# A ring of 512 points with the far pairs on VectorE, and a Fourier channel table with its high and low columns side by side

## The chip, the cores and the metric

The kernel runs on one core of a Trainium2 chip. The metric is the device time of one execution in microseconds (us), the median of three runs. TensorE is called PE here, its weight loads PEld; VectorE is DVE, ScalarE is ACT, GpSimd is POOL, SyncE is SP.

## The reference

One layer mixes 272 positions (16 learned meta tokens and 256 tokens) of width 2048. A wide projection feeds three branches of 1024 channels each; the branches are gated, projected back, weighted, summed, projected once more and added to the input, and a last RMSNorm follows. Branch A and branch B are what the change touches:

```python
def fftconv(v, kf, skip):                       # branch A, twice in a row
    L = v.shape[1]
    vf = jnp.fft.rfft(v.astype(jnp.float32), n=2 * L, axis=1)
    y = jnp.fft.irfft(vf * kf[None], n=2 * L, axis=1)[:, :L]
    return y + v.astype(jnp.float32) * skip.astype(jnp.float32)

def hyena_mixer(u, x1, x2, kf, skip):
    z = fftconv(u, kf[:, 0], skip[0])
    z = x1.astype(jnp.float32) * z
    z = fftconv(z, kf[:, 1], skip[1])
    z = x2.astype(jnp.float32) * z
    return z.astype(u.dtype)

def fourier_mixer(xb):                          # branch B, over 256 channels of a group and all positions
    B, L, C = xb.shape
    xg = xb.astype(jnp.float32).reshape(B, L, FN_GROUPS, C // FN_GROUPS)
    y = jnp.fft.fft2(xg, axes=(1, 3), norm='ortho').real
    return y.reshape(B, L, C).astype(xb.dtype)
```

The filter `kf` has 272 lags forward and 271 back. It comes from a small network over the positions, whose last layer `w4` gives 4096 columns, each multiplied by a decay `exp(-t * abs(decay))`. All is float32.

## The kernel before

**Number format.** PE multiplies numbers of a shorter format (F32R here). A float32 matrix is split into a high part, made by ACT (a copy into F32R), and a low part, made by DVE (the matrix less its high part). A product then takes three matmuls, high x high, low x high and high x low; the helper `three` issues them at L594 to L596, so these lines carry most of PE's work. The 16 rows or bins that go beyond 128 or 256 would need matmuls of their own; where they are rows of the contraction, their high, low and high parts are stacked under one another (rows 0, 32 and 64 of an 80-row tile) and one matmul covers them. The helper `stacked` issues it at L599.

**Main loop.** The channels go in 4 chunks of 256 (`c`), and a chunk has 20 steps (`t`). At each step one slab of projection weights (1 MB, loaded by SP into `raw`, four deep) is used: `split` makes `w_hi` on ACT and `w_lo` on DVE, two slabs ahead, and PE does 48 matmuls with it. Ten projections (`u`, `q`, `k`, `v`, `x1`, `x2`, three gates and the input of branch B) take two steps each. Between the slabs each engine has its share of the three branches at fixed places, written out by hand as `if t == ...` in one loop per engine; every engine works its list in that order and waits on semaphores. After the four chunks comes the merge: 512 columns wide, four blocks of 18 slabs, and the output projection with 16 slabs.

**Branch A.** The convolution is circular over a ring of 2 x 272 = 544 points, with 272 complex bins. For each of 8 groups `g` (2 per chunk, one per order of the convolution) the filter is made so: `make_h4(g, tt)` (L640, L641) runs the network's last layer for the lag tiles 0, 1 (128 lags each) and 2 (16 lags); `sum_and_difference` and `sd_low` on DVE and `envelope` and `sd_high` on ACT multiply it by the decay and split it; `filter_xy` transforms it to 256 bins, with a `stacked` matmul (out of `sd_rest`) for the 16 lags behind each `three`; `filter_f` (L669 to L674 and L599) makes the 16 bins that remain. The signal is folded (`fold`, DVE), transposed (`turn`, L717), transformed (`forward` for 256 bins, `forward_extra`, L736, L737 and L599, for the last 16), multiplied by the spectrum (`straight`, `crossed`, `spectrum_low` on DVE; f = 2 is the tile of 16 bins), and brought back (`inverse` with `wide_half`, L744 and L745, with one `stacked` matmul of 136 columns per accumulation for the 16 bins), then `unfold`.

**Branch B.** `fnet_channels(t, bank)` does the transform over channels by a table `fch` of cosines and sines with 130 columns per position tile (t = 0, 1): `three` matmuls for each half of the channels. `channels_high` (ACT) and `channels_low` (DVE) split the result, `fnet_tokens` transforms over positions.

**Where steps meet.** At t = 7 PE ends with `scores(0)` of the attention branch; DVE does `biased(c, 0)` on them, then `normalized(c, 0)` once ACT has taken exponentials, and copies the block `v` out of PSUM (L1632) during step 7 of its own list; PE transposes the probabilities (`turn_p`, L780, L782) and `v` (`turn`, L717) after the slab of t = 8. `crossed(2, 0, ...)` of the 16 bins stands ahead of `biased(c, 0)`, and its `spectrum_low` behind.

Of the kernel before, what the change touches and what calls it, by code (L numbers as in the profile page):

```python
# [35 lines left out]
L = 272  # L36
# [13 lines left out]
FFT_N = 2 * L  # L50
HL = L // 2

# [54 lines left out]
FPOS = np.concatenate([np.arange(256, L), np.arange(0, 256, 2), np.arange(1, 256, 2)])  # L107
FSTACK = 4 * 128 + 8 * NM
FWIDE = FSTACK + 4 * 128 + 2 * NM
# [24 lines left out]
def constants():  # L134

    pos = np.arange(L, dtype=np.float64)
    bins = np.concatenate([np.arange(128, 144), np.arange(128), np.arange(L - 1, 143, -1)]).astype(np.float64)
    om = TWO_PI * (bins + 0.5) / FFT_N
    sign = 1.0 - 2.0 * (bins % 2)

    half = (pos[:HL, None] + 0.5) * om[None, :]
    even = np.cos(half) + sign[None, :] * np.sin(half)
    odd = np.cos(half) - sign[None, :] * np.sin(half)
    none = np.zeros((HL - 128, L))
    back = [np.concatenate([even.T[p:p + n], odd.T[p:p + n]], axis=1) for p, n in TOK]
    hi, lo = two_parts(np.concatenate([even[:128], odd[:128], back[0], back[1]], axis=1),
                       np.concatenate([np.concatenate([even[128:], none]), np.concatenate([none, odd[128:]]), back[2]], axis=1))
    wide = [part[:, at:at + HL] for b in (2 * L, 3 * L) for part, at in ((hi, b), (lo, b), (hi, b + HL), (lo, b + HL))]
    extra_bins = [part[:, at:at + NM] for part in (hi, lo) for at in (0, L)]
    extra_rest = [np.pad(hi[:, at:at + NM], ((0, 0), (0, 2 * NM))) for at in (4 * L, 5 * L)]  # L150
    sym = (np.concatenate([hi[:, 0:2 * L]] + wide + [hi[:, 4 * L:]] + extra_bins + extra_rest, axis=1),
           lo[:, 0:2 * L])

    lag = FPOS.astype(np.float64)[:, None] * om[None, :]
    cosk, sink = np.cos(lag) / FFT_N, -np.sin(lag) * sign[None, :] / FFT_N
    first, extra = slice(NM, NM + 128), slice(0, NM)
    te, to, tr = slice(NM, NM + 128), slice(NM + 128, L), slice(0, NM)
    is_even = 1.0 - FPOS[tr, None] % 2
    filt = two_parts(np.concatenate([cosk[te, first], sink[te, first], cosk[to, first], sink[to, first],
                                     cosk[te, extra], sink[te, extra], cosk[to, extra], sink[to, extra]], axis=1),  # L160
                     np.concatenate([cosk[tr, first] * is_even, sink[tr, first] * is_even,
                                     cosk[tr, first] * (1.0 - is_even), sink[tr, first] * (1.0 - is_even),
                                     cosk[tr, extra], sink[tr, extra]], axis=1))

    hi, lo = filt
    more = [part[:, 512 + 2 * NM * tt:512 + 2 * NM * tt + 2 * NM] for tt in range(2) for part in (hi, lo)]
    filt = np.concatenate([hi[:, 0:512]] + more + [hi[:, 512 + 4 * NM:]], axis=1), lo[:, 0:512]
# [5 lines left out]
    fch = two_parts(np.concatenate([np.cos(ang), fsin], axis=1).reshape(2, 128, 2 * FK).transpose(1, 0, 2).reshape(128, -1), None)  # L173
# [16 lines left out]
    negt = np.zeros((128, 3), f32)  # L190
    for i, (p, n) in enumerate(TOK):
        negt[:n, i] = -t[FPOS[p:p + n], 0]
# [8 lines left out]
def build(nc, x, meta, w_stream, filt_in, sym_in, fch_in, ftok_in, net_in, negt_in, mask_in, ident_in, params_in, w4,  # L201
# [5 lines left out]
    def place(name, shape, dt=F32):  # L207
# [3 lines left out]
        return t  # L211


    params = place("params", [128, 128])
    ident = place("ident", [128, 128])
    negt = place("negt", [128, 3])
    mask = place("mask", [128, GRID_W])
# [118 lines left out]
    with ExitStack() as ctx:  # L336
# [253 lines left out]
        def _(pe):  # L590
# [34 lines left out]
            def make_h4(g, tt):  # L625
# [11 lines left out]
                if tt == 2:  # L637
                    pe.wait_ge(h4_read, 3 * g + 1)
# [1428 lines left out]
```

## Time and profile before

| | |
|---|---|
| runs of before | 1112.69, 1112.76, 1112.93 us (median 1112.76) |
| profiled execution: span from first to last instruction | 1111.3 us |
| profiled execution: around its span | the profile gives no time of its own for it; its span lies 1.46 us under the median |
| PE busy | 1092.6 us, 98% of the span, 7104 matmuls recorded |
| DVE busy | 785.6 us, 71% |
| ACT busy | 568.6 us, 51% |
| POOL busy | 67.0 us, 6% |
| DMA | 201.80 MB, mean 182 GB/s |

Matmuls overlap in the records: one lasts some 0.28 us from its start to its end, while the next starts after 0.11 to 0.23 us. What a matmul costs PE is therefore read from the distance between two starts, and not from its duration. Idle time of an engine costs something only where another engine waits for it; each instruction that had to wait carries the wait and what ended it.

### The profile page before, as it was taken

The page shows a single profiled execution, that of the slowest core. Times are in us where ns is not written, and L with a number is a line of the kernel's source. Part 1 is how long each engine was busy: PE and PEld are TensorE (multiplying, and loading weights), DVE is VectorE, ACT ScalarE, POOL GpSimd, SP SyncE. Part 2 cuts the span into 40 slices and gives each one's busy share as a digit, 9 for nine tenths or more (in the row PEclk, how much of TensorE's full clock was granted, in tenths as well). Part 3 has the DMA queues.
Part 4 walks back from the last instruction along what each step waited for, and adds up shares of the span by engine and source line. Part 5 has one row for each costly group of instructions (what it writes and reads, how often), then busy time and mean ns, then how long its engine had stood idle before and what let it go on. Part 6 is the DMA issues. An engine that isn't in the chain of part 4 may idle for free.

```text
span 1111.3 us, 17195 instructions
## 1 busy us (share of the span) xinstructions
PE 1092.6 (98%) x7104; PEld 1000.8 (90%) x7104; DVE 785.6 (71%) x1185; ACT 568.6 (51%) x794; POOL 67.0 (6%) x104
## 2 busy tenths in 40 slices
PE   5999999999999999999999999999999999999997
PEld 5999999999999999999999988888888888888886
DVE  7888888688897798986888785454555545554654
ACT  6755555456465556554655564444444444344543
POOL 5130000300003000002000000000000000000000
PEclk9999999999999999999999999999999999999999
DMA  9763443644344634354444575555555555557652
GB/s 353 253 189 123 152 145 131 208 171 150 117 161 165 205 124 152 132 175 178 149 140 149 187 252 192 197 183 198 200 199 184 197 190 189 189 190 269 223 192 111
DMA packets 30734, 201.80 MB, mean 182 GB/s; under 512 B 3905, under 2 KB 4289, under 8 KB 7969
## 3 DMA queue, kind: packets, MB, share of 16 engines
q1 hardware_dynamic: 25264, 180.34, 46.8%
q0 software_dynamic: 5248, 19.85, 5.5%
q8 instruction: 56, 0.92, 0.3%
q10 hardware_dynamic: 144, 0.52, 0.1%
q14 instruction: 22, 0.17, 0.1%
HBM read 195.46 MB, written 5.24 MB: 181 GB/s over the span
## 4 chain that ended last, share of the span: by engine, by line
PE 98%; DMA 1%; ACT 0%; SPq 0%; DVE 0%; issue 0%; ACTq 0%
PE ps L594 30%; PE ps L596 30%; PE ps L595 30%; PE ps L599 2%; PE ps L717 1%; PE ps L744 1%; DMA xin<-x 1%; PE ps L780 1%; PE ps L622 1%; PE ps L640 1%; PE ps L641 1%; PE ps L772 0%; PE ps L771 0%; PE ps L993 0%; PE ps L782 0%; PE ps L745 0%
## 5 line engine op out<-in xcount | busy, mean ns | idle before, releaser
L1413 DVE TENSOR_TENSOR w_lo<-raw,w_hi 128x1024 fp32r<-128x1024 f32 (+1 forms) x338 | 408.6, 1223 | 249.4 <-ACT w_hi L1051 247.4
L1051 ACT ACTIVATE w_hi<-raw 128x1024 fp32r<-128x1024 f32 x334 | 349.0, 1057 | 342.7 <-PE ps L596 341.6
L594 PE MATMUL ps<-xn_hi,w_hi 128*128 128x272 f32 (+2 forms) x1280 | 367.9, 287 | 0.0
L596 PE MATMUL ps<-xn_hi,w_lo 128*128 128x272 f32 (+2 forms) x1280 | 365.0, 285 | 0.0
L595 PE MATMUL ps<-xn_lo,w_hi 128*128 128x272 f32 (+2 forms) x1280 | 364.8, 285 | 0.0
L594 PEld LDWEIGHTS ps<-xn_hi,w_hi 128*128 128x128 f32 x1280 | 241.6, 189 | 2.5 <-DVE xn_lo L1468 0.4
L595 PEld LDWEIGHTS ps<-xn_lo,w_hi 128*128 128x128 f32 x1280 | 241.2, 188 | 0.7
L596 PEld LDWEIGHTS ps<-xn_hi,w_lo 128*128 128x128 f32 x1280 | 241.5, 189 | 0.0
L594 PE MATMUL ps<-w_hi,xg_hi 128*128 128x512 f32 x352 | 137.2, 390 | 0.0
L596 PE MATMUL ps<-w_hi,xg_lo 128*128 128x512 f32 x352 | 137.0, 389 | 0.0
L595 PE MATMUL ps<-w_lo,xg_hi 128*128 128x512 f32 x352 | 136.9, 389 | 0.0
L596 PEld LDWEIGHTS ps<-w_hi,xg_lo 128*128 128x128 f32 x352 | 66.1, 188 | 13.8
L595 PEld LDWEIGHTS ps<-w_lo,xg_hi 128*128 128x128 f32 x352 | 66.1, 188 | 13.6
L594 PEld LDWEIGHTS ps<-w_hi,xg_hi 128*128 128x128 f32 x352 | 66.1, 188 | 13.5
L594 PE MATMUL ps<-w_hi,yb_hi 128*128 128x512 f32 x192 | 74.8, 389 | 0.0
L596 PE MATMUL ps<-w_hi,yb_lo 128*128 128x512 f32 x192 | 74.7, 389 | 0.0
L595 PE MATMUL ps<-w_lo,yb_hi 128*128 128x512 f32 x192 | 74.7, 389 | 0.0
L1267 ACT ACTIVATE y_hi<-prod 128x512 fp32r<-128x512 f32 (+1 forms) x24 | 15.2, 632 | 70.2 <-DVE prod L1698 70.1
L594 PE MATMUL ps<-w_hi,m_hi 128*128 128x512 f32 x128 | 49.9, 390 | 0.0
L596 PE MATMUL ps<-w_hi,m_lo 128*128 128x512 f32 x128 | 49.8, 389 | 0.0
L595 PE MATMUL ps<-w_lo,m_hi 128*128 128x512 f32 x128 | 49.8, 389 | 0.0
L594 PEld LDWEIGHTS ps<-w_hi,yb_hi 128*128 128x128 f32 x192 | 36.0, 188 | 7.6 <-issue 0.2
(292 smaller groups left out, 1388.2 us busy)
## 6 DMA issues: line engine op xcount, KB each, us to landing
raw<-w_stream SPq DMA_DIRECT2D x167, 1024.0 KB, 4.9
branch_y<-ystage POOLq DMA_DIRECT2D x12, 256.0 KB, 4.0
y_raw<-branch_y POOLq DMA_DIRECT2D x3, 1024.0 KB, 7.1
xin<-x SPq DMA_DIRECT2D x2, 1024.0 KB, 6.4
w4s<-w POOLq DMA_DIRECT2D x16, 128.0 KB, 5.6
absd<-decay POOLq DMA_DIRECT2D x8, 256.0 KB, 5.8
h<-x POOLq DMA_DIRECT2D x2, 1024.0 KB, 8.3
rows_t<-rpb POOLq DMA_DIRECT2D x8, 219.0 KB, 6.2
```

The lines of the kernel that those rows point to most:

```text
L594: mm(out_ap, a_hi, b_hi, start=first, stop=False)
L595: mm(out_ap, a_hi, b_lo, start=False, stop=False)
L596: return mm(out_ap, a_lo, b_hi, start=False, stop=last)
L599: return mm(out_ap, a, b, start=first, stop=last)
L622: last = nc.tensor.transpose(ps[:, 4 + k % 4, p:p + 128], xin[:, t, 128 * k:128 * k + 128], ident[:, :])
L640: mm(out_ap, hid_s[:, p:p + n], w4_hi[:, :, :].rearrange("p d n -> p (d n)"), start=True, stop=False)
L641: mm(out_ap, hid_s[:, p:p + n], w4_lo[:, :, :].rearrange("p d n -> p (d n)"), start=False, stop=True).then_inc(h4_mm, 1)
L717: last = nc.tensor.transpose(dst, src[:, i, p:p + n], ident[:, :])
L744: mm(ps[:, bank, 0:L], y_hi[:, f, ri, chans], sym_hi[:, back:back + L], start=f == 0, stop=False)
L1051: A(w_hi[:, w % 2, part, :], raw[:, w % 4, 1024 * part:1024 * part + 1024], ACT.Copy).then_inc(hi_done, 1)
L1267: ins = A(y_hi[0:n, f, :, :], prod[0:n, 2, :, :], ACT.Copy)
L1413: return V.tensor_tensor(dst, src, hi.bitcast(F32), ALU.subtract)
```

## The change

Branch A goes over to a ring of 512 points. Then 256 bins do, and the last tile of 16 bins and its table columns disappear. On that ring the pairs of positions that are 256 to 271 apart wrap and would be counted at a wrong lag, so the ring's filter holds lags 0 to 255 only (`filter_xy` loses its `stacked` matmuls) and the far pairs are summed directly: 16 x 16 products on each side for every channel. `far_lags(g)` on PE (two matmuls for each of 4 outputs, of 32 columns, with a 128-column stationary operand out of `w4_hi` or `w4_lo`) makes the filter at 32 lags with channels on the partitions; `far_envelope` (ACT, 4 small exponentials, with the decay as a scale per partition) and `far_kernel` (DVE) weight it and add what the ring wrapped; `far_terms(order, src)` on DVE multiplies by a view of it shaped like a Toeplitz matrix (128 x 512) and sums along rows (a reduce of 512 elements to 32); `unfold` adds the 16 positions at either end. In order 1 only the later positions are needed.

In branch B the table's high and low columns stand side by side (`fch_two`, 260 wide), so the high part of the input takes one matmul of 260 columns in place of two of 130, into two ranges of the bank. Those two must be added: ACT copies one out of PSUM (`fch_sum`), DVE adds the other, and the split is made from the sum.

Tables loaded at the start change in size: `fch` doubles (1032 and 1040 columns where there were twice 516), `filt` goes from 1184 + 512 to 512 + 512 columns, `sym` from 2608 + 544 to 2112 + 512. ACT takes the absolute value of a 32-column block of `params` once, just behind `hid_s` and ahead of `envelope(0, 0)`, and DVE sets one column of `hid_s` to zero.

The diff, cut to what runs:

```diff
             def filter_xy(g):
-                pe.wait_ge(sdlo_done, 3 * g + 2)
+                pe.wait_ge(sdlo_done, 2 * g + 2)
                 pe.wait_ge(h4_read, 3 * g + 3)
                 for ri in range(2):
-                    into = [ps[:, 7 - tt, CC * ri:CC * ri + CC] for tt in range(2)]
                     for tt in range(2):
                         col = 256 * tt + 128 * ri
-                        three(into[tt], filt_hi[:, col:col + 128], filt_lo[:, col:col + 128], sd_hi[:, tt, ri, :],
-                              sd_lo[:, tt, ri, :], True, False)
-                    if ri == 0:
-                        pe.wait_ge(sdlo_done, 3 * g + 3)
-                    for tt in range(2):
-                        col = FSTACK + 256 * tt + 128 * ri
-                        last = stacked(into[tt], filt_hi[0:STACK, col:col + 128], sd_rest[0:STACK, ri, :], False, True)
+                        last = three(ps[:, 7 - tt, CC * ri:CC * ri + CC], filt_hi[:, col:col + 128], filt_lo[:, col:col + 128],
+                                     sd_hi[:, tt, ri, :], sd_lo[:, tt, ri, :], True, True)
...
+            def far_lags(g):
+                pe.wait_ge(h4_read, 3 * g + 1)
+                for d in range(2):
+                    for i in range(2):
+                        out_ap = ps[:, 6, 2 * NM * (2 * d + i):2 * NM * (2 * d + i) + 2 * NM]
+                        chans = slice(128 * i, 128 * i + 128)
+                        mm(out_ap, w4_hi[:, d, chans], hid_s[:, 0:2 * NM], start=True, stop=False)
+                        last = mm(out_ap, w4_lo[:, d, chans], hid_s[:, 0:2 * NM], start=False, stop=True)
+                last.then_inc(h4_mm, 1)
...
             def wide_half(bank, ri, chans):
                 for f in range(2):
...
-                rest = 8 * L + HL * ri
-                return stacked(ps[:, bank, 0:HL], y_hi[0:STACK, 2, ri, chans], sym_hi[0:STACK, rest:rest + HL], False, True)
...
             def fnet_channels(t, bank):
...
-                    last = three(ps[0:n, bank, cols], fi_hi[:, i, p:p + n], fi_lo[:, i, p:p + n], fch_hi[:, i, cols],
-                                 fch_lo[:, i, cols], i == 0, i == 1)
+                    at_ = 2 * (FK + 1) * t
+                    mm(ps[:, bank, 0:2 * (FK + 1)], fi_hi[:, i, p:p + n], fch_two[:, i, at_:at_ + 2 * (FK + 1)], start=i == 0, stop=False)
+                    last = mm(ps[:, bank, 0:FK + 1], fi_lo[:, i, p:p + n], fch_two[:, i, at_:at_ + FK + 1], start=False, stop=i == 1)
...
                     if t == 2:
-                        make_h4(2 * c + 1, 2)
+                        far_lags(2 * c + 1)
                     if t == 4:
                         filter_xy(2 * c + 1)
-                    if t == 5:
-                        filter_f(2 * c + 1)
...
-                    if t == 5:
-                        pe.wait_ge(y_full, c * 6 + 1)
-                        forward_extra()
...
+            def far_envelope(g):
+                if g:
+                    act.wait_ge(h4_read, 3 * g)
+                c, o_ = divmod(g, 2)
+                for d in range(2):
+                    for i in range(2):
+                        at_ = DEC + 8 * (2 * o_ + d) + 2 * c + i
+                        ins = A(far_env[:, d, i, :], negt[:, 2:2 + 2 * NM], ACT.Exp, scale=params[:, at_:at_ + 1])
+                ins.then_inc(env_done, 1)
...
+            def far_kernel(g):
+                o_ = g % 2
+                dve.wait_ge(env_done, 3 * g + 3)
+                dve.wait_ge(h4_mm, 3 * g + 3)
+                V.tensor_tensor(far[:, :, :, :].rearrange("p d i n -> p (d i n)"), ps[:, 6, 0:8 * NM],
+                                far_env[:, :, :, :].rearrange("p d i n -> p (d i n)"), ALU.mult).then_inc(h4_read, 1)
+                dve.wait_ge(h4_read, 3 * g + 3)
+                if g == 0:
+                    dve.wait_ge(far_zeroed, 1)
+                link(V.tensor_tensor(far_k[:, o_, :, :, NM - 1:2 * NM - 1], far[:, :, :, 0:NM], far[:, ::-1, :, NM:2 * NM], ALU.add))
...
+            def far_terms(order, src):
+                ins = V.tensor_tensor(far_p[:, 0, :, :, :], toeplitz(order, 0, True), spread(src, 0), ALU.mult)
+                if order:
+                    link(ins)
+                else:
+                    link(V.tensor_tensor(far_p[:, 1, :, :, :], toeplitz(order, 1, False), spread(src, NB), ALU.mult))
+                    link(V.tensor_reduce(far_y[:, 1, :, :], far_p[:, 1, :, :, :], mybir.AxisListType.X, ALU.add))
+                link(V.tensor_reduce(far_y[:, 0, :, :], far_p[:, 0, :, :, :], mybir.AxisListType.X, ALU.add))
...
             def channels_high(f, second):
                 if not second:
                     for r in range(2):
-                        half = slice(FK * r, FK * r + FK)
                         act.wait_ge(n1_mm, f * 3 + r + 1)
-                        A(p2_hi[:, r, half], ps[:, 4 + r, half], ACT.Copy).then_inc(n1_hi, 1)
+                        A(fch_sum[:, r, :], ps[:, 4 + r, FK + 1:2 * FK + 2], ACT.Copy).then_inc(n1_part, 1)
+                    for r in range(2):
+                        act.wait_ge(n1_sum, f * 2 + r + 1)
+                        A(p2_hi[:, r, FK * r:FK * r + FK], fch_sum[:, r, r:r + FK], ACT.Copy).then_inc(n1_hi, 1)
...
             def channels_low(f, second):
                 if not second:
                     for r in range(2):
+                        dve.wait_ge(n1_part, f * 2 + r + 1)
+                        V.tensor_tensor(fch_sum[:, r, :], fch_sum[:, r, :], ps[:, 4 + r, 0:FK + 1], ALU.add).then_inc(n1_sum, 1)
+                    for r in range(2):
                         dve.wait_ge(n1_hi, f * 3 + r + 1)
...
                     if t == 6:
-                        crossed(2, 0, straight(c, 2, 0))
                         biased(c, 0)
-                        spectrum_low(c, 2, 0)
+                        far_terms(0, u)
                         normalized(c, 0)
...
                     if t == 13:
-                        crossed(2, 1, straight(c, 2, 1))
                         turned(c * HC + 4, pt_hi, pt_lo, pT_lo[:, :, :], pT_hi[:, :, :], pT_rest, 6, NG, 32)
                         attended(c, 2)
-                        spectrum_low(c, 2, 1)
+                        far_terms(1, x1)
```

What stands on PE behind the slab of t = 5 in the first chunk before (`filter_f`, then `forward_extra`), between two slabs' matmuls:

```order
L596 MATMUL ps<-xn_hi,w_lo 128x272
L669 MATMUL ps<-sd_hi,filt_hi 48x256
L670 MATMUL ps<-sd_lo,filt_hi 16x256
L599 MATMUL ps<-sd_rest,filt_hi 16x256
L673 MATMUL ps<-sd_lo,filt_hi 16x256
L674 MATMUL ps<-sd_hi,filt_hi 48x256
...
L736 MATMUL ps<-uT_hi,sym_hi 48x256
L737 MATMUL ps<-uT_lo,sym_hi 16x256
L599 MATMUL ps<-uT_hi,sym_hi 48x256
...
L594 MATMUL ps<-xn_hi,w_hi 128x272
```

In the changed kernel nothing is left there: the slab of t = 6 follows that of t = 5. The new matmuls on PE stand behind the slab of t = 2, where before the two of the 16-lag tile stood (`w_hi` and `w_lo` are `w4_hi` and `w4_lo` by the names here); the changed kernel has there:

```order
L593 MATMUL ps<-xn_hi,w_lo 128x256
L645 MATMUL ps<-hid_s,w_hi 128x32
L646 MATMUL ps<-hid_s,w_lo 128x32
L645 MATMUL ps<-hid_s,w_hi 128x32
L646 MATMUL ps<-hid_s,w_lo 128x32
...
L591 MATMUL ps<-xn_hi,w_hi 128x256
```

Two matmuls of 512 columns became eight of 32 columns, each with its own weights.

On DVE at t = 6 of the first chunk, before (L1744 is `biased`, L1751 and L1753 are `normalized`, L1632 is the copy of `v`):

```order
L1687 TENSOR_TENSOR extra<-extra,ps 16x512
L1691 TENSOR_TENSOR prod<-extra,kspec 16x512
L1696 TENSOR_TENSOR prod<-extra,kspec 16x512
L1697 TENSOR_TENSOR prod<-prod 16x256
L1698 TENSOR_TENSOR prod<-prod 16x256
...
L1747 TENSOR_SCALAR stat<-stat 128x2
L1413 TENSOR_TENSOR y_hi<-prod,y_hi 16x512
L1751 RECIPROCAL stat<-stat 128x2
L1753 TENSOR_SCALAR sco<-sco,stat 128x272 x2
L1413 TENSOR_TENSOR w_lo<-raw,w_hi 128x1024
L1632 COPY v<-ps 128x544
```

and in the changed kernel:

```order
L1703 TENSOR_SCALAR stat<-stat 128x2
L1512 TENSOR_TENSOR far_p<-far_k,u 128x512
L1516 TENSOR_TENSOR far_p<-far_k,u 128x512
L1517 TENSOR_REDUCE far_y<-far_p 128x32
L1518 TENSOR_REDUCE far_y<-far_p 128x32
L1707 RECIPROCAL stat<-stat 128x2
L1709 TENSOR_SCALAR sco<-sco,stat 128x272 x2
L1359 TENSOR_TENSOR w_lo<-raw,w_hi 128x1024
L1595 COPY v<-ps 128x544
```

Five instructions ahead of `biased` are gone, and the one between `biased` and `normalized` has become four.

## Rows read from the trace of the kernel before

**Rows 1.** The profile's page: busy time of the engines, and the chain that ended last.

```profile
PE 1092.6 (98%) x7104; PEld 1000.8 (90%) x7104; DVE 785.6 (71%) x1185; ACT 568.6 (51%) x794; POOL 67.0 (6%) x104
...
PE 98%; DMA 1%; ACT 0%; SPq 0%; DVE 0%; issue 0%; ACTq 0%
```

**Rows 2.** The waits of PE: us in total, times, longest.

```profile
PE ps L610 <- DMA net<-net_in: 7.6, 1, 7.6
PE ps L834 <- ACT ps L1063: 3.9, 1, 3.9
```

**Rows 3.** Busy time by stretch, the second chunk; behind POOL the granted clock (PEclk).

```profile
207.00:354.00 147.00, 147.00 (x1205) 145.45 (x1204) 124.01 (x226) 83.40 (x136) 10.37 (x17) 1.00 0.47 158
```

**Rows 4.** Timeline of PE at `filter_f`, first and last start (start, duration in us).

```profile
209.06 0.28 PE L669 MATMUL ps<-sd_hi,filt_hi 128*48 128x256 f32 x1
...
210.24 0.29 PE L594 MATMUL ps<-xn_hi,w_hi 128*128 128x272 f32 x1
```

**Rows 5.** Timeline of PE at `forward_extra`.

```profile
246.82 0.28 PE L736 MATMUL ps<-uT_hi,sym_hi 128*48 128x256 f32 x1
...
247.53 0.29 PE L594 MATMUL ps<-xn_hi,w_hi 128*128 128x272 f32 x1
```

**Rows 6.** Timeline of PE at the 16-lag tile of `make_h4`.

```profile
222.90 0.40 PE L640 MATMUL ps<-w_hi,hid_s 128*16 128x512 f32 x1
...
223.37 0.28 PE L594 MATMUL ps<-xn_hi,w_hi 128*128 128x256 f32 x1
```

**Rows 7.** Timeline of PE at one pair of `stacked` matmuls in `filter_xy`.

```profile
236.46 0.41 PE L599 MATMUL ps<-sd_rest,filt_hi 80*128 80x256 f32 x2
236.71 0.28 PE L594 MATMUL ps<-sd_hi,filt_hi 128*128 128x256 f32 x1
```

**Rows 8.** Timeline of PE in `inverse`, a run of 136-column matmuls.

```profile
124.79 0.27 PE L599 MATMUL ps<-sym_hi,y_hi 80*128 80x136 f32 x1
...
125.01 0.28 PE L595 MATMUL ps<-sym_hi,y_hi 128*128 128x136 f32 x1
```

**Rows 9.** Groups by form on PE: busy us, mean ns of one.

```profile
L745 PE MATMUL ps<-sym_hi,y_lo 128*128 128x136 f32 x48 | 10.9, 226 | 0.0
...
L596 PE MATMUL ps<-sym_hi,y_lo 128*128 128x136 f32 x16 | 4.4, 276 | 0.0
```

**Rows 10.** Groups by form of weight loads: 128 and 16 stationary columns.

```profile
L596 PEld LDWEIGHTS ps<-sym_hi,y_lo 128*128 128x128 f32 x16 | 3.1, 192 | 0.0
...
L596 PEld LDWEIGHTS ps<-fch_hi,fi_lo 128*16 128x16 f32 x8 | 0.8, 95 | 0.2
```

**Rows 11.** Groups by form on DVE, a product of 512 elements in SBUF.

```profile
L1880 DVE TENSOR_TENSOR u<-u,x 128x512 f32<-128x512 f32 x4 | 2.7, 685 | 0.0
```

**Rows 12.** Timeline of DVE at t = 6 and 7, second chunk.

```profile
261.69 0.17 DVE L1747 TENSOR_SCALAR stat<-stat 128x2 f32<-128x2 f32 x1
...
263.41 0.17 DVE L1751 RECIPROCAL stat<-stat 128x2 f32<-128x2 f32 x1 [0.46 <-ACT sco L1275]
263.61 0.63 DVE L1753 TENSOR_SCALAR sco<-sco,stat 128x272 f32<-128x272 f32 x2
264.37 1.23 DVE L1413 TENSOR_TENSOR w_lo<-raw,w_hi 128x1024 fp32r<-128x1024 f32 x1
265.51 0.72 DVE L1632 COPY v<-ps 128x544 f32<-128x544 f32 x1
```

**Rows 13.** Timeline of PE there: behind `scores(0)`, and `turn(v)`.

```profile
260.13 0.29 PE L594 MATMUL ps<-xn_hi,w_hi 128*128 128x272 f32 x1
...
266.83 0.71 PE L717 MATMUL ps<-ident,v 128*128 128x128 f32 x5
```

**Rows 14.** Timeline at the start, DVE's low part of slab 4.

```profile
47.22 1.22 DVE L1413 TENSOR_TENSOR w_lo<-raw,w_hi 128x1024 fp32r<-128x1024 f32 x1
```

**Rows 15.** Timeline of PE there, the first matmul with slab 4.

```profile
48.59 0.36 PE L594 MATMUL ps<-xn_hi,w_hi 128*128 128x272 f32 x1
```

**Rows 16.** Groups by form on ACT, its smallest copy of all 128 partitions.

```profile
L1220 ACT ACTIVATE k_hi<-k_hi 128x64 fp32r<-128x64 f32 x4 | 1.0, 257 | 0.1
```

More of the change, by code:

```diff
@@ L49 @@
 HID, EMB = 64, 33
[L50 removed]
+RING = 512
+NB = RING // 2
 HL = L // 2
+LF = L + NM
+HF = LF // 2
 TOK = [(NM, 128), (NM + 128, 128), (0, NM)]
@@ L136, in constants @@
     pos = np.arange(L, dtype=np.float64)
[L137 to L163, printed above, removed]
@@ L165, in constants @@
-    hi, lo = filt
-    more = [part[:, 512 + 2 * NM * tt:512 + 2 * NM * tt + 2 * NM] for tt in range(2) for part in (hi, lo)]
-    filt = np.concatenate([hi[:, 0:512]] + more + [hi[:, 512 + 4 * NM:]], axis=1), lo[:, 0:512]
+    bins = np.concatenate([np.arange(128), np.arange(NB - 1, 127, -1)]).astype(np.float64)
+    om = TWO_PI * (bins + 0.5) / RING
+    turn = np.where(bins < 128, 1.0, -1.0)
+    half = (pos[:HL, None] - (L - 1) / 2) * om[None, :]
+    even = np.cos(half)
+    odd = -np.sin(half) * turn[None, :]
@@ new lines, in constants @@
+    none = np.zeros((HL - 128, NB))
+    back = [np.concatenate([even.T[p:p + 128], odd.T[p:p + 128]], axis=1) for p in (0, 128)]
+    hi, lo = two_parts(np.concatenate([even[:128], odd[:128]] + back, axis=1),
+                       np.concatenate([np.concatenate([even[128:], none]), np.concatenate([none, odd[128:]])], axis=1))
+    wide = [part[:, at:at + HL] for b in (BACK, BACK + L) for part, at in ((hi, b), (lo, b), (hi, b + HL), (lo, b + HL))]
+    sym = np.concatenate([hi[:, 0:BACK]] + wide + [hi[:, BACK + 2 * L:]], axis=1), lo[:, 0:BACK]
@@ L169, in constants @@
+    lag = np.arange(NB, dtype=np.float64)[:, None] * om[None, 0:128]
+    cosk, sink = np.cos(lag) / NB, -np.sin(lag) / NB
+    filt = two_parts(np.concatenate([cosk[0::2], sink[0::2], cosk[1::2], sink[1::2]], axis=1), None)
     ch = np.arange(CC, dtype=np.float64)
@@ L172, in constants @@
     fsin[:, [0, FK - 1]] = 0.0
-    fch = two_parts(np.concatenate([np.cos(ang), fsin], axis=1).reshape(2, 128, 2 * FK).transpose(1, 0, 2).reshape(128, -1), None)
+    both = np.concatenate([np.cos(ang), fsin], axis=1).reshape(2, 128, 2 * FK).transpose(1, 0, 2)
+    hi, lo = two_parts(both.reshape(128, -1), None)
+    hi, lo = hi.reshape(128, 2, 2 * FK), lo.reshape(128, 2, 2 * FK)
+    pairs = [np.concatenate([part[:, :, cols] for part in (hi, lo)], axis=2) for cols in (slice(0, FK + 1), slice(FK - 1, 2 * FK))]
+    fch = np.concatenate(pairs, axis=2).reshape(128, -1), np.concatenate([hi, lo], axis=2).reshape(128, -1)
     angl = TWO_PI * ((pos[:, None] * pos[None, NM:]) % L) / L
@@ L659, in filter_xy @@
                         if ri == 1:
                             last.then_inc((kx_mm, ky_mm)[tt], 1)
-            def filter_f(g):
-                bank = 7
-                pe.wait_ge(kx_evac, g + 1)
-                for ri in range(2):
-                    out_ap, wide_ap = (ps[0:n, bank, CC * ri:CC * ri + CC] for n in (NM, 3 * NM))
-                    col, step = 512 + NM * ri, 4 * NM
-                    mm(wide_ap, filt_hi[:, col:col + 3 * NM], sd_hi[:, 0, ri, :], start=True, stop=False)
-                    mm(out_ap, filt_hi[:, col:col + NM], sd_lo[:, 0, ri, :], start=False, stop=False)
-                    stacked(out_ap, filt_hi[0:STACK, FSTACK + col:FSTACK + col + NM], sd_rest[0:STACK, ri, :], False, False)
-                    col += step
-                    mm(out_ap, filt_hi[:, col:col + NM], sd_lo[:, 1, ri, :], start=False, stop=False)
-                    last = mm(wide_ap, filt_hi[:, col:col + 3 * NM], sd_hi[:, 1, ri, :], start=False, stop=True)
-                last.then_inc(kf_mm, 1)
@@ L849, in _ @@
             proj_half(3, 2, 1, NM, 0)
-            make_h4(0, 2)
+            far_lags(0)
             proj_half(3, 2, 1, NM, 1)
@@ L963, in _ @@
                         if t == 17:
-                            make_h4(2 * c + 2, 2)
+                            far_lags(2 * c + 2)
                         if t == 19:
```

298 lines of the change are left out of this document (120 added, 178 removed).

## The prediction

> **What bounds the kernel now.** I read the page first: PE is busy for 1092.6 us of 1111.3, and the chain that ended last lies on PE for 98% of the span [rows 1]. The waits of PE say where the rest is: 7.6 and 3.9 us at the start, for the first transfers and the first squares, and not one wait behind them [rows 2]. What is left is the tail behind the last matmul. The table by stretch shows the same for one chunk: PE has no idle time in 147 us, DVE is busy for 124.0 of them and ACT for 83.4, at a granted clock of 1.00, which is the 2.4 GHz level [rows 3]. So the time is the sum of the distances between the starts of matmuls. A matmul taken away gives its distance back, a matmul added costs its distance, and work of DVE and ACT costs nothing as long as no wait of PE comes of it. I therefore price the PE edits by starts in the timeline, and then look for the places where PE now comes earlier or DVE later.
>
> **What PE loses.** There are 8 groups of filters and 8 convolutions (4 chunks x 2).
> - `filter_f`: 10 matmuls from 209.06 to 210.24, 1.18 us [rows 4], times 8: 9.4 us. The 16 or 48 stationary columns make them no cheaper; they move 256 columns.
> - `forward_extra`: 6 matmuls, 246.82 to 247.53, 0.71 us [rows 5], times 8: 5.7 us.
> - the 16-lag tile of `make_h4`: 222.90 to 223.37, 0.47 us [rows 6], times 8: 3.8 us.
> - `stacked` in `filter_xy`: a pair takes 0.25 us [rows 7], two pairs for each group, 16 in all: 3.9 us.
> - `stacked` in `inverse`: two steps in a run of 136-column matmuls take 0.22 us, 0.11 each [rows 8], 8 for each chunk, 32 in all: 3.5 us.
> - `fnet_channels`: a `three` of 130 columns is priced like three of 136, 0.33 us [rows 8]. One of its matmuls goes, and another grows from 130 to 260 columns, for which I take the 0.12 us of a 256-column matmul (ten in 1.18 us, [rows 4]). So 0.33 becomes 0.12 + 0.11 = 0.23. Two tiles, two halves, four chunks: 16 x 0.10 = 1.6 us.
>
> Together 27.9 us.
>
> **What PE gains.** `far_lags` adds 64 matmuls (8 for each group) that move 32 columns only. No row shows one so narrow. From below: if only the moved columns counted, the step from 512 columns (0.235 us, half of 0.47) to 256 (0.118) gives 0.46 ns a column, so 0.015 us, and 64 of them 1 us. From above: a run of 136-column matmuls takes 0.11 us each [rows 8], 7.0 us for 64; I know of no reason why 32 columns should take longer than 136. I take the upper end, for what limits those runs is not the columns. The same 136 columns last 226 ns where a 272-column matmul precedes each one, and 276 ns in a run of their own kind [rows 9]: in the run each stands 50 ns waiting for something that a longer predecessor hides. Its weights are that: a load of 128 stationary columns takes 192 ns, one of 16 takes 95 [rows 10], so 0.87 ns a column and 0.11 us for 128, the distance in the run. All `far_lags` matmuls have 128 stationary columns, new ones each time. **Sum for PE: 27.9 - 7.0 = 20.9 us less.**
>
> The Trainium skill has a rule for each end, on the page "TensorE: Matmul & The Clock Gate". Its section "Back-to-back issue gap" puts a matmul of 1 to 64 columns at a floor of about 25 ns; an estimate from that is 1.6 us for the 64 instead of 7.0. Its section "LDWEIGHTS (loading the stationary operand)" puts a load at its columns divided by 1.2, 107 ns for 128, which would give 6.8 us. The trace's 136-column runs agree with the second; none of its rows is narrow enough to refute the first.
>
> **What DVE and ACT do, and who waits.** Everything that goes from DVE and ACT worked on 16 partitions but lasted as long as on 128. A product of 512 elements in SBUF takes 0.685 us on DVE [rows 11], and for each group seven such instructions and four of half the size go; for each chunk three products and three reduces of 512 come, with small additions. DVE's sum per chunk falls by some 6 us, PE's by 5.2. So DVE keeps its distance as a whole, and only single meetings can turn bad. These I went through one by one: the folded signal, the transposed signal, the probabilities and the weight slabs keep a lead, mostly because `filter_step` on DVE and ACT has less to do ahead of them. Two places are near.
>
> First, `v` at t = 8. `biased(c, 0)` cannot start before PE's `scores(0)` is done at 260.13 [rows 13]. Today DVE comes late to it, since `crossed` of the 16 bins stands ahead, and ends it at 261.86 [rows 12]. In the changed kernel DVE is waiting there, and ends about 0.2 + 1.0 us behind the scores, at 261.3 on the same clock of PE. Then come the four instructions of `far_terms`: at 0.685 each, with 0.035 for the wait between linked ones and some overlap at the first, 2.75 us, to 264.05. `normalized` takes 0.8 (263.41 to 264.24, [rows 12]), so the next `w_lo` starts near 264.85 (264.37 today), and the copy of `v`, today 265.51 to 266.23, ends 1.14 + 0.72 us later, at 266.7. PE wants it at 266.83 [rows 13]. The lead shrinks from 0.6 us to 0.1 or 0.2. Mirrored and repeated access patterns and the reduce itself have no row of this size; from below they cost what the product costs, from above twice that. I take the product's price: no wait.
>
> Second, the start. The low part of slab 4 is ready at 48.44 [rows 14], and PE begins with it at 48.59 [rows 15]: PE is held by DVE here. ACT's new absolute value, ahead of the envelopes and so of the splits behind them, moves that chain. 32 columns lie under the 0.257 us of 64 [rows 16]; I take 0.25 us with the longer MLP columns, between 0 and 0.5. On PE `far_lags(0)` comes 0.4 us later out, `fnet_channels` 0.4 us sooner. I book 0.25 us lost. The doubled `fch` table, `filt` and `sym` together stay about as large as before and are asked for long before PE reads them; cover gone would cost the lateness itself, which I put at nothing.
>
> **The sum.** 20.9 - 0.25, about 20.6 us. The profiled span of 1111.3 goes to 1090.7, and with the 1.46 us by which it lies under the median, to 1092.1 us.
>
> **Rivals.**
> - *Narrow matmuls are cheap.* If the 64 cost 0.025 us or less, 5.4 us more is gained: 1086.7. For it: no row under 128 columns. Against it: [rows 8 to 10]. Chance 0.08.
> - *The reduce or the mirrored product is slow, and `v` is late.* If each reduce takes twice 0.685, DVE is 1.4 us later with 0.15 of lead, so about 1.2 us in three chunks and less in the first, whose lead is larger: some 4 us, 1096. The page "VectorE: DVE Perf Modes" of the Trainium skill, section "Rules for kernel authors", calls `tensor_reduce` the slowest operation of VectorE but puts it at one element a cycle, the rate of the float32 product. Chance 0.10.
> - *Slower than before: DVE becomes the bound behind the scores.* This asks for a delay there of over 5.2 us per chunk beyond the lead, that is `far_terms(0)` of over 8.1 us where I count 2.75, an average of 2.0 us for each instruction, three times the price of [rows 11]. With four times the price it is 11 us, (11 - 2.9) x 4 = 32 us of waits against 21 gained: 1124. Chance 0.02.
> - *The change gives nothing, as PE waits for what it saved.* DVE at 84% of a chunk [rows 3] leaves no room for that as a sum; it would take a new order of waits at nearly every step. Chance 0.02, near 1112.
>
> The forecast itself gets 0.78: 1092.1, and alone 1090.5 to 1094. The range for 8 in 10 reaches part of the way to both rivals, 1089 to 1096: in it lie the forecast and most of the slow reduce. A difference of 0.2%, 2.2 us, is about what can be told from none: faster by more 0.96, within it 0.02, slower 0.02.
>
> **What would show it.** PE with 6944 matmuls or so in the records, again without waits behind the start, and a chunk 5.2 us shorter by its starts. Eight `far_lags` matmuls in 0.88 us, 0.11 apart. On DVE products and reduces of `far_terms` near 0.69 us. `v` ready 0.1 to 0.2 us ahead of `turn(v)`. I am wrong if the narrow matmuls stand 0.03 apart, if PE shows waits for DVE at `turn(v)` or at `turn_p`, or if the start loses more than 0.5 us.

## The result, and the profile of the changed kernel

The changed kernel takes 1096.85 us (median of 4 runs, 1096.76 to 1097.73) against 1112.85 us before (4 runs): a ratio of 0.9858, 95% interval 0.9844 to 0.9872. It is faster by 16.0 us, 1.4%. The prediction said 1092.1 us with a range to 1096.0, so the time lies outside it, 4.7 us above the forecast.

The page of the changed kernel, whose profiled execution has a span of 1095.1 us, answers to [rows 1]:

```profile
PE 1072.8 (98%) x6944; PEld 982.1 (90%) x6944; DVE 764.3 (70%) x1158; ACT 542.8 (50%) x779; POOL 67.9 (6%) x104
...
PE 94%; DVE 3%; ACT 1%; DMA 1%; issue 0%; SPq 0%; ACTq 0%
```

The 6944 matmuls are those that were forecast. The chain of work that ended last is the first sign: before it lay on PE for 98%, now 3% of it are DVE's, some 33 us. PE waits for something that DVE makes, and the chain runs back over DVE from there. The waits of PE (us in total, times, longest) answer to [rows 2] and name it:

```profile
PE ps L607 <- DMA net<-net_in: 7.3, 1, 7.3
PE ps L809 <- ACT ps L1028: 3.8, 1, 3.8
PE ps L717 <- DVE o L1721: 3.7, 3, 1.2
PE ps L591 <- DVE xn_lo L1414: 0.3, 1, 0.3
```

The third row is new, three times 1.2 us (the fourth, 0.3 us once, lies at the start, at 24.85, and comes and goes between executions: far_early, below, has none, narrow_96 has 0.4). In the third row L717 is the first matmul of a `wide_half` and L1721 is VectorE's addition in `attended`. In the code it is this line of `inverse(c, 1)`, at t = 15:

```python
                    if order:
                        if i:
                            pe.wait_ge(o_done, c * HC + 4)
                        last = wide_half(6 + i, 1, chans)
```

PE may not write bank 7 before VectorE has added the result that `attend(3)` left there. The change does not touch these lines. The timeline of PE (start, duration in us, idle time before and what ended it) shows the place in the first chunk:

```profile
166.47 0.23 PE L718 MATMUL ps<-sym_hi,y_lo 128*128 128x136 f32 x1
166.53 0.34 PE L717 MATMUL ps<-sym_hi,y_hi 128*128 128x272 f32 x1
166.71 0.22 PE L718 MATMUL ps<-sym_hi,y_lo 128*128 128x136 f32 x1
168.16 0.39 PE L717 MATMUL ps<-sym_hi,y_hi 128*128 128x272 f32 x1 [1.23 <-DVE o L1721]
```

From 166.71 to 168.16 are 1.45 us where such a step takes 0.06 (166.47 to 166.53). The same stands in the second and third chunk (1.45 us at 312.73 and 458.74), and in the last chunk it is 0.26. In the run far_early below, where nothing is waited for here, this step is 0.06, and the one behind it is 0.06 shorter too. So the wait costs 1.45 us in each of three chunks and 0.26 in the last, 4.6 us.

A second, smaller delay follows at t = 16, where `make_h4` (L634) asks for the unfolded signal. The view of waits doesn't list it, but the starts show it:

```profile
174.30 0.28 PE L593 MATMUL ps<-xn_hi,w_lo 128*128 128x256 f32 x1
174.61 0.50 PE L634 MATMUL ps<-w_hi,hid_s 128*128 128x512 f32 x1
```

VectorE ends the unfolding at 174.55, and PE's step to L634 is 0.31 us, where it was 0.12 in the kernel before (178.58 to 178.70, with the unfolding done at 178.56) and is 0.15 in far_early. Against far_early PE loses 0.16 to 0.20 us there in three chunks, 0.5 in all. With the 4.6 that is 5.1 us, against a distance of 4.8 between the medians of the two kernels; in the profiled executions the changed kernel was 0.4 us ahead of far_early at its first `turn(v)` (113.08 and 113.51).

What VectorE did meanwhile:

```profile
160.68 0.69 DVE L1359 TENSOR_TENSOR pT_lo<-ps,pT_hi 128x512 fp32r<-128x512 f32 x1 [2.84 <-ACT pT_rest L1195]
161.38 0.41 DVE L1359 TENSOR_TENSOR pT_rest<-ps,pT_rest 16x256 fp32r<-16x256 f32 x1
161.83 0.41 DVE L1721 TENSOR_TENSOR o<-o,ps 64x256 f32<-64x256 f32 x1
162.17 0.68 DVE L1512 TENSOR_TENSOR far_p<-far_k,x 128x512 f32<-128x512 f32 x1
162.88 0.69 DVE L1518 TENSOR_REDUCE far_y<-far_p 128x32 f32<-128x512 f32 x1
163.60 3.45 DVE L1359 TENSOR_TENSOR w_lo<-raw,w_hi 128x1024 fp32r<-128x1024 f32 x2
166.98 0.41 DVE L1572 COPY fi<-ps 128x256 f32<-128x256 f32 x1
167.31 0.15 DVE L1573 COPY fi<-ps 128x14 f32<-128x14 f32 x1
167.50 0.16 DVE L1574 COPY fi<-ps 128x4 f32<-128x4 f32 x1
167.68 0.42 DVE L1721 TENSOR_TENSOR o<-o,ps 64x256 f32<-64x256 f32 x1
```

And GpSimd (POOL) at the same time:

```profile
164.24 1.73 POOL L554 TENSOR_TENSOR w_lo<-w4s,w_hi 128x512 fp32r<-128x512 f32 x1 [90.22 <-ACT w_hi L1076]
```

The same work in the kernel before, VectorE from 167.11 and GpSimd:

```profile
167.11 0.41 DVE L1765 TENSOR_TENSOR o<-o,ps 64x256 f32<-64x256 f32 x1
167.55 0.68 DVE L1413 TENSOR_TENSOR y_hi<-prod,y_hi 16x512 fp32r<-16x512 f32 x1
168.34 2.36 DVE L1413 TENSOR_TENSOR w_lo<-raw,w_hi 128x1024 fp32r<-128x1024 f32 x2
170.62 0.42 DVE L1609 COPY fi<-ps 128x256 f32<-128x256 f32 x1
...
171.69 0.42 DVE L1765 TENSOR_TENSOR o<-o,ps 64x256 f32<-64x256 f32 x1 [0.37 <-ACT o L1254]
```

```profile
170.82 1.28 POOL L557 TENSOR_TENSOR w_lo<-w4s,w_hi 128x512 fp32r<-128x512 f32 x1 [95.03 <-ACT w_hi L1111]
```

Before, VectorE was idle for 0.37 us ahead of the fourth addition: it was released by ScalarE's copy, and ended at 172.11, and PE's matmul that asks for it started at 172.38, a lead of 0.27 us. After, VectorE has no idle time but some hundredths of a microsecond between instructions from 160.68 to the end of the unfolded signal at 174.55, which PE asks for next. Two things stand in that queue. The far product and reduce take 1.40 us where the low part of the 16-bin spectrum took 0.68. And the two splits of the weights take 3.45 us instead of 2.36: the second begins at 164.74 and lasts 2.31 us instead of 1.22, while GpSimd makes the next chunk's `w4_lo`. Before, GpSimd's 1.28 us lay beside VectorE's `fi` copies, and neither was longer for it. It has moved ahead of them because ScalarE, without the 16-bin spectra, makes `w4_hi` sooner: 3.26 us behind its last copy of the probabilities (160.27 to 163.53) where it was 4.56 (165.55 to 170.11), the two copies `y_hi<-prod` of 16 bins between them, 1.3 us together, being gone.

The idle 2.84 us in the first row are the way out: VectorE waits there for the probabilities, and `far_terms(1, x1)`, whose inputs have long been there, stands behind them.

### The profile page after: what moved, and what is told of

Same layout as the page of the kernel before. It is cut to its first block, busy times and chain, and to the rows that moved or that the text cites. A ratio compares the mean times of both kernels' runs of the same rounds, so it can differ in the third digit from the quotient of the medians.

```text
span 1095.1 us, 16828 instructions
## 1 busy us (share of the span) xinstructions
PE 1072.8 (98%) x6944; PEld 982.1 (90%) x6944; DVE 764.3 (70%) x1158; ACT 542.8 (50%) x779; POOL 67.9 (6%) x104
## 4 chain that ended last, share of the span: by engine, by line
PE 94%; DVE 3%; ACT 1%; DMA 1%; issue 0%; SPq 0%; ACTq 0%
PE ps L591 29%; PE ps L593 29%; PE ps L592 29%; DVE w_lo L1359 1%; PE ps L701 1%; PE ps L751 1%; DMA xin<-x 1%; PE ps L596 1%; PE ps L717 0%; PE ps L634 0%; PE ps L743 0%; PE ps L742 0%; PE ps L635 0%; PE ps L646 0%; PE ps L753 0%; PE ps L958 0%
## 5 line engine op out<-in xcount | busy, mean ns | idle before, releaser
L593 PEld LDWEIGHTS ps<-w_hi,yb_lo 128*128 128x128 f32 x192 | 36.0, 188 | 7.5
```

What stands on the lines that cost most here:

```text
L593: return mm(out_ap, a_lo, b_hi, start=False, stop=last)
```

## The experiments

**Far terms into the idle time.** Base is the changed kernel, as in all that follow unless another is named.

```diff
                     if t == 13:
+                        far_terms(1, x1)
                         turned(c * HC + 4, pt_hi, pt_lo, pT_lo[:, :, :], pT_hi[:, :, :], pT_rest, 6, NG, 32)
                         attended(c, 2)
-                        far_terms(1, x1)
```

> Base is the changed kernel; at t = 13 VectorE now does far_terms(1, x1) ahead of the turned probabilities instead of behind attended(c, 2), so its product and reduce (about 1.4 us) lie in the 2.8 us in which VectorE waits for ScalarE there. Theory A (the missing 4.7 us are TensorE's wait at t = 15 for o_done, that is for VectorE's addition attended(c, 3), which is late because 1.4 us of far_terms stand ahead of it and because a weight split is stretched from 1.22 to 2.31 us while GpSimd computes w4_lo): the splits start 1.4 us sooner, the addition is done before TensorE asks, all four waits (3 x 1.33 + 0.2 us) go, time 1092.3 us, 4 to 5 us under the changed kernel. Rival B (the missing time is in the narrow products or in matmuls that cost more than forecast, and the wait only takes the place of another one right behind it): within 1 us of the changed kernel's 1096.9.

Measured: 1092.07 us (1091.98 to 1092.32), ratio to before 0.9813 (0.9798 to 0.9827). That is 4.8 us under the changed kernel. The waits of PE are those of the start alone again:

```profile
PE ps L607 <- DMA net<-net_in: 7.3, 1, 7.3
PE ps L809 <- ACT ps L1028: 3.8, 1, 3.8
```

And the addition is released by ScalarE's copy again, as before the change:

```profile
158.21 0.69 DVE L1512 TENSOR_TENSOR far_p<-far_k,x 128x512 f32<-128x512 f32 x1
158.93 0.69 DVE L1518 TENSOR_REDUCE far_y<-far_p 128x32 f32<-128x512 f32 x1
161.19 0.69 DVE L1359 TENSOR_TENSOR pT_lo<-ps,pT_hi 128x512 fp32r<-128x512 f32 x1 [1.58 <-ACT pT_rest L1195]
...
166.51 0.42 DVE L1721 TENSOR_TENSOR o<-o,ps 64x256 f32<-64x256 f32 x1 [0.36 <-ACT o L1211]
```

It ends at 166.93, and PE goes through the place without a halt:

```profile
167.15 0.22 PE L718 MATMUL ps<-sym_hi,y_lo 128*128 128x136 f32 x1
167.22 0.34 PE L717 MATMUL ps<-sym_hi,y_hi 128*128 128x272 f32 x1
```

Theory A holds. Rival B falls: nothing of its size took the wait's place (PE's step to L634 at t = 16 is 0.15 us here, 0.03 above that of the kernel before). No version of the study is faster than this one by more than the spread of its runs.

**The addition first.** A fix of a different kind, on the queue just ahead of the wait.

```diff
                     if t == 15:
+                        attended(c, 3)
                         if c < LAST:
                             fin_mirrors(c, 7)
-                        attended(c, 3)
-                        if c < LAST:
                             fold_fin(c, 7)
```

> Base is the changed kernel; at t = 15 VectorE does attended(c, 3) ahead of fin_mirrors(c, 7), nothing else moves. Theory A: the addition comes 0.70 us sooner in three chunks, TensorE's wait there falls from 1.33 to about 0.6 us in each, the last chunk (which has no fin_mirrors) stays: 2.0 us faster, 1094.9 us. If fin_mirrors in its turn made the next block of fin late, less. Rival B: no change.

Measured: 1097.89 us (1097.11 to 1098.23), 1.0 above the changed kernel, whose runs reach up to 1097.73. A miss by 3 us, and the most instructive one. Its waits of PE behind the start:

```profile
PE ps L634 <- DVE u L1685: 2.2, 3, 0.8
PE ps L717 <- DVE o L1721: 1.9, 3, 0.6
```

The wait for the addition is down from 1.2 to 0.6 us in each chunk, as expected. But what PE gained it lost at t = 16, where `make_h4` waits for the unfolded signal. VectorE has no idle time between the two, so a new order of its work moves the time from one wait to the next and shortens nothing. It even costs VectorE 0.12 us: the addition starts 0.03 behind the end of the second split, where the `fi` copy of the changed kernel started 0.07 before it (166.98 and 167.05). Of the 1.0 us by which it is slower, the distance between `turn(v)` in two chunks accounts for 0.5 (146.17 instead of 146.02 us, three times). The rest lies ahead of the first `turn(v)`, at 113.66 instead of 113.08, where nothing was changed: the profiled executions whose work is the same up to there have it anywhere from 112.95 (narrow_96) to 113.66, and both_moves at 114.35, because its first matmul waited 8.2 us for its table and not 7.3.

**GpSimd later.**

```diff
                 pool.wait_ge(w4hi_done, 2 * c + 3)
+                pool.wait_ge(o_done, (c + 1) * HC)
                 nc.gpsimd.tensor_tensor(w4_lo[:, :, :], w4s[:, :, :], w4_hi[:, :, :].bitcast(F32), ALU.subtract).then_inc(w4lo_done, 1)
```

> Base is the changed kernel; GpSimd's subtraction that makes w4_lo for the next chunk (1.73 us, beside a VectorE split of 2.31 us where others take 1.22) waits until VectorE's fourth addition is done. Theory A with contention between the two engines as its larger half: the split takes 1.22 us again, the addition comes 1.09 us sooner in three chunks, 3.2 us faster, 1093.7 us; w4_lo is ready some 5 us before TensorE wants it. Rival A2 (the split is long for another reason, the far product alone made the addition late): the split stays at 2.3 us and the time within 0.5 us of the changed kernel.

Measured: 1095.05 us (1094.84 to 1095.22), 1.8 us faster, not 3.2. VectorE and GpSimd in it:

```profile
163.98 2.36 DVE L1360 TENSOR_TENSOR w_lo<-raw,w_hi 128x1024 fp32r<-128x1024 f32 x2
...
168.38 1.53 DVE L1360 TENSOR_TENSOR w_lo<-raw,w_hi 128x1024 fp32r<-128x1024 f32 x1
```

```profile
167.54 1.28 POOL L555 TENSOR_TENSOR w_lo<-w4s,w_hi 128x512 fp32r<-128x512 f32 x1 [93.15 <-DVE o L1722]
```

The two splits take 2.36 us again and GpSimd's subtraction 1.28, so rival A2 falls: the split was long because of GpSimd. The 1.09 us came, but the subtraction now collides with the next split, which lasts 1.53 us instead of 1.22, and VectorE stays without idle time. 1.09 - 0.31 = 0.78 us for each of three chunks would be 2.3; the distance between `turn(v)` in two chunks is 0.72 shorter (145.30), and this profiled execution was 0.4 us behind that of the changed kernel at the first one (113.44). The expectation had priced the wait and not the queue behind it, as in the run before.

**Both.** far_early with GpSimd's new wait as well.

> far_early and pool_later together: far_terms(1, x1) in the idle time ahead of the turned probabilities, and GpSimd's w4_lo behind VectorE's fourth addition. Theory A: with far_terms moved the addition and the unfolded signal are in time, so taking the contention away as well gives nothing: 1092.1 us, within 0.3 us of far_early. If VectorE were still late somewhere in this stretch, up to 1 us faster.

Measured: 1093.0 us (1092.7 to 1094.15), 0.9 slower than far_early. Nothing to gain was right, nothing to lose was not. `w4_lo` comes beside the split at t = 15, which lasts 1.53 us here too, and PE waits for the unfolded signal behind it. A chunk is 0.3 us longer (144.73 instead of 144.43 between two `turn(v)`, the mean of three), which makes the 0.9. All of the 0.31 us by which the split is longer shows, so in far_early the unfolded signal has no slack left. There GpSimd's subtraction (164.68 to 166.18) falls mostly beside the `fi` copies and costs VectorE nothing.

**GpSimd in two halves.** To see how the two engines hinder each other.

```diff
-                nc.gpsimd.tensor_tensor(w4_lo[:, :, :], w4s[:, :, :], w4_hi[:, :, :].bitcast(F32), ALU.subtract).then_inc(w4lo_done, 1)
+                for d in range(2):
+                    ins = nc.gpsimd.tensor_tensor(w4_lo[:, d, :], w4s[:, d, :], w4_hi[:, d, :].bitcast(F32), ALU.subtract)
+                ins.then_inc(w4lo_done, 1)
```

> Base is the changed kernel; GpSimd makes w4_lo in two instructions of 256 elements instead of one of 512, nothing is moved. In the changed kernel GpSimd's instruction lasts 1.73 us where it takes 1.28 with no split beside it, and ends at 165.97; VectorE's second split, 1.22 us elsewhere, lasts until 167.05, which is 1.08 after that. Theory L (each of the two engines waits for the whole instruction of the other): VectorE gets in between the two halves, its split ends some 0.5 us sooner, about 1.8 instead of 2.3 us, and as VectorE has no idle time up to the unfolded signal, the chunk is 0.5 us shorter: three chunks, 1.5 us, 1095.4 us. Theory B (the two share the memory in proportion and slow each other down as long as both run): halves change nothing, the split stays at 2.3 us, the time within 0.4 us of 1096.9. The Trainium skill, page "SBUF — State Buffer", section "Who interferes with whom", has the first as its rule: an exclusive lock for the whole instruction, when VectorE has two inputs in SBUF and GpSimd reads SBUF.

Measured: 1095.61 us (1095.25 to 1095.79), 1.2 us faster; a chunk is 0.53 us shorter (145.49 instead of 146.02). VectorE's two splits, and GpSimd:

```profile
163.77 2.90 DVE L1361 TENSOR_TENSOR w_lo<-raw,w_hi 128x1024 fp32r<-128x1024 f32 x2
```

```profile
164.41 2.85 POOL L555 TENSOR_TENSOR w_lo<-w4s,w_hi 128x256 fp32r<-128x256 f32 x2 [90.24 <-ACT w_hi L1078]
```

The second split lasts 1.76 us instead of 2.31. The single starts and ends show the turns: VectorE's first split ends at 165.00, GpSimd's first half at 165.59, 0.59 later, VectorE's second split at 166.67, 1.08 after that, and GpSimd's second half at 167.26, 0.59 after that. Theory L holds, and theory B, by which halves change nothing, falls.

**The ring part alone.** The changed kernel with the Fourier channel table, `fnet_channels`, `channels_high` and `channels_low` as in the kernel before.

> The changed kernel with the Fourier channel table as before (three matmuls 129 columns wide for each half instead of one of 260 and one of 130, no addition by VectorE): only the ring part of the change is left. The prediction priced the Fourier part at 16 x 0.10 = 1.6 us of TensorE time: then 1098.5 us. A rival, that the addition by VectorE ahead of the split of the channel sums costs as much as it gives: 1096.9, no change.

Measured: 1098.44 us (1098.24 to 1098.73), 1.6 above the changed kernel. The Fourier part is worth what it was priced at, 0.43 us for each chunk (146.45 instead of 146.02 between two `turn(v)`), and VectorE's additions in it cost nothing that shows.

**The price of a narrow matmul.** Two kernels on far_early.

```diff
-                for d in range(2):
+                for d in (0, 1, 0, 1):
```

> Base is far_early. Each far_lags does its eight 32-column matmuls twice over (the second pass writes the same values), 64 more in all. If such a matmul costs what the trace shows from start to start (94 to 112 ns, the price of bringing in 128 fresh columns of weights), 7.0 us more: 1099.1 us. If it costs what its 32 columns do at the rate of the 272-column products, about 1 us more: 1093.1 us. A part of it may be hidden where TensorE would have waited anyway (0.2 us).

Measured: 1099.07 us (1098.89 to 1099.16), 7.0 more.

```diff
-                        out_ap = ps[:, 6, 2 * NM * (2 * d + i):2 * NM * (2 * d + i) + 2 * NM]
+                        out_ap = ps[:, 6, 2 * NM * (2 * d + i):2 * NM * (2 * d + i) + 6 * NM]
                         chans = slice(128 * i, 128 * i + 128)
-                        mm(out_ap, w4_hi[:, d, chans], hid_s[:, 0:2 * NM], start=True, stop=False)
-                        last = mm(out_ap, w4_lo[:, d, chans], hid_s[:, 0:2 * NM], start=False, stop=True)
+                        mm(out_ap, w4_hi[:, d, chans], hid_s[:, 0:6 * NM], start=True, stop=False)
+                        last = mm(out_ap, w4_lo[:, d, chans], hid_s[:, 0:6 * NM], start=False, stop=True)
```

> Base is far_early. The eight matmuls of far_lags move 96 columns of hid_s instead of 32 (the surplus columns are overwritten by the next product or read by nobody). If the floor is the weight load, the 64 more columns are free: 1092.1 us. If the columns moved set the price, 64 x 64 columns at some 0.42 ns (the 272-column product takes 0.12 us) are 1.7 us more: 1093.8 us.

Measured: 1092.05 us (1091.83 to 1092.98), as far_early. So 64 narrow matmuls cost 7.0 us, 0.11 each, and 64 more columns in each cost nothing: the columns moved are not what limits them. The timeline of the changed kernel, matmuls and weight loads (PEld), showed the distance already:

```profile
182.93 0.18 PE L645 MATMUL ps<-hid_s,w_hi 128*128 128x32 f32 x1
182.96 0.26 PE L646 MATMUL ps<-hid_s,w_lo 128*128 128x32 f32 x1
183.07 0.26 PE L645 MATMUL ps<-hid_s,w_hi 128*128 128x32 f32 x1
183.18 0.26 PE L646 MATMUL ps<-hid_s,w_lo 128*128 128x32 f32 x1
```

```profile
182.82 0.19 PEld L645 LDWEIGHTS ps<-hid_s,w_hi 128*128 128x128 f32 x1
182.93 0.19 PEld L646 LDWEIGHTS ps<-hid_s,w_lo 128*128 128x128 f32 x1
183.04 0.19 PEld L645 LDWEIGHTS ps<-hid_s,w_hi 128*128 128x128 f32 x1
```

From 182.93 to 182.96 are 0.03 us. The weights of the first matmul were brought in beside the last wide one (from 182.82), and it lasts 0.18 us; the second starts close behind it but lasts 0.26, since its own load only began at 182.93. Every later step is 0.11, the distance between two loads, and the `three` behind the eight loses the 0.08 back (its first step is 0.20 instead of 0.12). So eight of them cost 0.90 us, and the short first step saves nothing. In narrow_96 that first step is 0.05: it alone feels the 64 columns.

**The lead of `v`.** Base is far_early.

```diff
                         biased(c, 0)
+                        link(V.tensor_tensor(far_p[:, 0, :, :, :], toeplitz(0, 0, True), spread(u, 0), ALU.mult))
                         far_terms(0, u)
```

> Base is far_early. At t = 6 VectorE does the first far product of far_terms(0, u) twice (0.68 us more in each of four chunks), ahead of normalized(c, 0), the two splits and v. The transposes of v start 0.06 us after VectorE's copy ends in every chunk, which is what a signal takes: v is at the edge, TensorE just waits for it. Then nearly all of it shows: 4 x 0.65 = 2.6 us more, 1094.7 us. If there were slack behind it (TensorE not really waiting), no change.

Measured: 1095.14 us (1094.69 to 1096.08), 3.1 more. PE waits for `v` four times:

```profile
PE ps L701 <- DVE v L1595: 2.3, 4, 0.6
```

A chunk is 0.72 us longer (145.17 instead of 144.45 between two `turn(v)`), the whole product with its link; four times 0.73 at `turn(v)` are 2.9 us. There was no slack left at `v`.

## Why the prediction was wrong, step by step

- **What PE loses and gains.** Right to the microsecond. With the wait for the addition gone in far_early a chunk takes 144.45 us between two `turn(v)`, 5.17 less than the 149.62 before, where 5.2 were forecast; and far_early takes 1092.07 us where 1092.1 was forecast. That it fits to a tenth is in part luck: PE still loses some 0.07 us at `v` and 0.1 at the unfolded signal in a chunk, for which the sum had nothing, and gains that much more elsewhere. The 7.0 us for `far_lags` are confirmed by adding 64 more, the 1.6 us of `fnet_channels` by taking that part back.
- **The step that failed** stands in the part on VectorE and ScalarE: "These I went through one by one: the folded signal, the transposed signal, the probabilities and the weight slabs keep a lead, mostly because `filter_step` on DVE and ACT has less to do ahead of them. Two places are near." The list lacked two meetings, the fourth addition (`o_done`, t = 15) and the unfolded signal (t = 16). These were two more near places, with 0.27 and 0.14 us of lead before (the signal itself takes 0.06 of that), and they cost 4.6 and 0.5 us. There the argument for the others turns round: at t = 13 `filter_step` does nothing, and what VectorE has in hand is `far_terms(1, x1)`, 1.40 us in place of a `spectrum_low` of 0.68. The 16-bin products that went had stood ahead of the probabilities, in time that VectorE now spends idle. Less work in the sum, more of it behind the last thing waited for.
- **"DVE's sum per chunk falls by some 6 us, PE's by 5.2. So DVE keeps its distance as a whole, and only single meetings can turn bad."** True as a sum (VectorE is busy for 785.6 us before and 761.6 in far_early, 6.0 less for each chunk), and no help for the stretch from 160.68 to 174.55, where VectorE is the bound with no idle time.
- **What was not thought of: GpSimd.** ScalarE's lost work moved GpSimd's subtraction 1.3 us forward, onto a split. Of the 4.8 us that far_early gives back, pool_later gives 1.8 by taking this collision away alone, though it buys a smaller one.
- **`v` at t = 8.** The mechanism was right, the lead over-rated: 0.1 to 0.2 us forecast, none measured. In the changed kernel the copy of `v` ends at 259.04 and the first transpose starts at 259.10, which is the time that a signal takes (168.10 to 168.16 at the wait of t = 15). It costs little because it is met almost exactly: the steps before and behind that start are 0.12 and 0.16 us where all others of the run are 0.11, 0.07 us in each of four chunks. Products and reduces took 0.68 to 0.69 us as priced, so the rival of a slow reduce, whose time of 1096 us the result nearly met, was not the cause: a number that fits is no mechanism.
- **The start.** The 0.25 us booked there can't be told from the differences of 0.7 us between executions up to the first `turn(v)`. It stays open.

## What to carry to other kernels

Where one engine sets the time, list every wait that it makes, from the code and not from memory, with its lead in the trace; for each, add up what the producer has to do between the last thing that it itself waits for and the signal. Work taken away ahead of that point gives nothing, and work that replaces it behind the point costs in full. And when an engine that is not the bottleneck loses work, look at what it triggers on a third one, and beside what that will then run; if two waits in a row are fed by an engine that has no idle time between them, only less work or work moved into its idle time helps, not another order.

## What the runs showed of the hardware

VectorE's subtraction with both inputs in SBUF (`w_lo<-raw,w_hi`, 1.22 us) and GpSimd's (`w_lo<-w4s,w_hi`, 1.28 us) exclude each other for the length of an instruction. In the changed kernel GpSimd's is issued at 164.24, beside a split that ends at 164.82, and ends at 165.97, 1.15 us after that end; VectorE's next split ends 1.08 us after that, at 167.05. The same 1.08 us stand in add_first, pool_later, both_moves and pool_halves, wherever a split had to follow GpSimd. With two halves the engines take turns, as above. VectorE's copies and additions that read PSUM are not hindered and don't hinder: 1.28 us for GpSimd and 0.42, 0.17 and 0.16 for the `fi` copies beside it in the kernel before. This agrees with the Trainium skill, page "SBUF — State Buffer", section "Who interferes with whom", which has the same condition (two inputs in SBUF on the one side, a read of SBUF on the other) and calls it an exclusive lock. The prediction, which used the Trainium skill for the narrow matmul, did not look there.

A matmul of 32 or 96 moved columns with 128 fresh stationary ones has a step of 0.11 us at the granted clock of 1.00 (2.4 GHz). Only the 0.03 us between the first two, ahead of which the weights of the first had been brought in beside a wide matmul, is near the floor of about 25 ns that the section "Back-to-back issue gap" of the Trainium skill's page "TensorE: Matmul & The Clock Gate" gives for narrow ones; the steps behind it follow the load of the weights. The same section says that in a stream of loads and matmuls both set the spacing, and the prediction's sentence on the 25 ns left that out.
